# A decoder step on one Trainium2 core: the input projection as one object across five attention stages

## The reference, cut to what matters

```python
u = rms_norm(x, lp['norm_g'][0])
nq, nkv, ngate, sz, sxbc, sdt, dqkv, mg = split_in(u @ lp['w_in'])   # one combined projection
# A: native sparse attention (compressed, selected, window) from nq, nkv, ngate
# B: Mamba-2 SSD mixer from sz, sxbc, sdt;   C: dilated window attention from dqkv
gates = jax.nn.sigmoid(mg.reshape(B, T, 3, D_MODEL))
mix = (gates[:, :, 0] * o_a + gates[:, :, 1] * o_b + gates[:, :, 2] * o_cc) @ lp['w_out']
```

## The kernel before

| stage | dense units before | what runs beside it |
|---|---|---|
| cmp | 36 (NSA columns) | compression of the caches |
| nsas | 72 (dilated columns) | sparse attention of the samples |
| dilp | 36 (SSD columns) and 27 (gates) | dilated attention of the prompt, cache copies |
| ssd | 18 (gates) | SSD mixer in 9 chunks, after a set-up of its own, cache copies |
| nsap | 27 (gates) | sparse attention of the prompt, small copies |

## Time and profile before

### The profile page before, as it was taken

One profiled execution on the slowest core, in us unless ns is written; L12 is line 12 of the kernel. 1 busy time (PEld: TensorE's weight loads), 2 busy tenths in 40 slices (PEclk: granted clock), 3 DMA queues, 4 the chain that ended last, 5 costly groups with the idle time before them and its releaser, 6 DMA issues. The chain is left out here.

```text
span 4517.3 us, 40132 instructions
## 1 busy us (share of the span) xinstructions
PE 3375.6 (75%) x13663; PEld 2097.3 (46%) x13663; DVE 1168.4 (26%) x2988; ACT 698.1 (15%) x1690; POOL 465.5 (10%) x317
## 2 busy tenths in 40 slices
PE   4699568687999545568887013996824999998999
PEld 2577445455555333234554012643412666665443
DVE  2011001012332155334543122412323232232000
ACT  1011000001111123123332001101102111111000
POOL 0000000000000032210000233010031011110000
PEclk7799779898999778679898555997656999999999
DMA  3443232313322258431000533322024111112100
GB/s 105 82 99 69 71 90 75 102 48 118 88 81 68 62 168 278 157 89 32 19 30 25 197 134 110 122 98 69 5 95 143 40 38 38 38 38 93 64 28 12
DMA packets 334815, 374.57 MB, mean 83 GB/s; under 512 B 57633, under 2 KB 297378, under 8 KB 330999
## 3 DMA queue, kind: packets, MB, share of 16 engines
q1 hardware_dynamic: 318162, 308.06, 22.8%
q10 hardware_dynamic: 16478, 64.32, 4.3%
HBM read 313.53 MB, written 115.44 MB: 95 GB/s over the span
## 5 line engine op out<-in xcount | busy, mean ns | idle before, releaser
L225 PE MATMUL d_ps<-d_w,mixer_u_T 128*128 128x288 f32 (+4 forms) x2304 | 675.2, 444 | 90.2 <-ACT d_ob L245 43.3
L2615 PE MATMUL ffn_ps<-up_u_T,ffn_w 128*128 128x352 f32 x2112 | 633.0, 461 | 0.0
L225 PEld LDWEIGHTS d_ps<-d_w,mixer_u_T 128*128 128x128 f32 (+1 forms) x2304 | 423.0, 191 | 276.2 <-issue 50.7
L2615 PEld LDWEIGHTS ffn_ps<-up_u_T,ffn_w 128*128 128x128 f32 x2112 | 400.7, 191 | 220.6 <-issue 2.0
L229 PE MATMUL d_ps<-mixer_u_T,d_w 128*128 128x352 f32 x1152 | 405.8, 499 | 19.0 <-DMA d_w<-w_in 19.0
L2496 PE MATMUL down_ps<-down_w,feed_g_T 128*128 128x512 f32 (+1 forms) x792 | 343.3, 596 | 17.9 <-DMA down_w<-ffn_w_down 17.9
L229 PEld LDWEIGHTS d_ps<-mixer_u_T,d_w 128*128 128x128 f32 x1152 | 225.0, 206 | 145.5 <-issue 44.4
L2496 PEld LDWEIGHTS down_ps<-down_w,feed_g_T 128*128 128x128 f32 (+1 forms) x792 | 144.4, 183 | 216.2 <-issue 198.0
L245 DVE COPY d_ob<-d_ps 128x352 f32<-128x352 f32 (+6 forms) x107 | 52.5, 491 | 444.6 <-PE d_ps L225 185.3
L2675 DVE TENSOR_SCALAR ffn_c<-ffn_h,ffn_now 128x1072 f32<-128x1072 f32 x44 | 36.8, 837 | 449.9 <-ACT ffn_h L2643 449.9
L2412 PE MATMUL mix_B<-gates_o_T,mix_wb 128*128 128x352 f32 x480 | 144.9, 466 | 10.3 <-DMA mix_wb<-w_br_c 10.3
(11 more groups left out here) (423 smaller groups left out, 3639.4 us busy)
## 6 DMA issues: line engine op xcount, KB each, us to landing
out_dil_sample<-cache_dil_w ACTq DMA_DIRECT2D x8, 4088.0 KB
ffn_w<-ffn_w_up SPq DMA_DIRECT2D x44, 512.0 KB, 4.8
cmp_rows<-cache_nsa_kv SPq DMA_DIRECT2D x128, 128.0 KB
dils_kv<-cache_dil_w SPq DMA_DIRECT2D x16, 1024.0 KB, 20.3
graw<-d_ob SPq DMA_DIRECT2D x72, 176.0 KB, 1.8
mix_gate<-graw SPq DMA_DIRECT2D x24, 528.0 KB, 5.6
d_w<-w_in SPq DMA_DIRECT2D x24, 512.0 KB, 6.7
dils_qb<-proj SPq DMA_DIRECT2D x3, 4096.0 KB, 23.2
```

What stands on the lines that cost most here:

```text
L225: mm = pe.matmul(ps[u % 2][0:rows, 0:cols], u_T[:, k, r0:r0 + rows], view(i)[:, k, :], start=(k == 0), stop=(k == DK - 1))
L2615: mm = pe.matmul(ps[u][:, 0:chunk], w[:, slot, k, a, :], u_T[:, k, x * chunk:(x + 1) * chunk], start=(k == 0), stop=(k == DK - 1))
```

## The change

- One object `Dense` holds the weights' slots, the ring, the PSUM tiles, the semaphores and the list of all 216 units; `lane(n)` hands out the next n units to a stage. Its load of the next block goes on over the end of a stage.
- A dense unit is 8 steps (each matmul a step) in place of 2.
- A gate block is 2 blocks of 128 columns (2 DMAs, 6 units), not 3 (3 DMAs, 9 units).
- Units by stage: 36, 72, 36, 36, 36 in place of 36, 72, 63, 18, 27.
- The programs of SP and POOL are run to their first `yield` ahead of all steps, so each attention lane's first loads stand ahead of dense in the queue. One `yield` more in each of these programs keeps the rest in place.
- The attention lane's steps take 0.1 to 0.98 in nsas and 0.08 to 1 in dilp and nsap; cmp and ssd stay at 0 to 1.

```diff
-    def turns(eng, programs):
+    def turns(eng, programs, early=False):
         own = [program(eng) if program else iter(()) for program in programs]
+        if early:
+            for program in own:
+                next(program, None)
...
-            turns(pool, [lane.pool for lane, _, _ in plan])
+            turns(pool, [lane.pool for lane, _, _ in plan], True)
...
-            turns(sp, [lane.sp for lane, _, _ in plan])
+            turns(sp, [lane.sp for lane, _, _ in plan], True)
...
+class Dense:
...
+    RING = 4
...
+        self.units = [(i, j) for i, (kind, _, _) in enumerate(parts) for j in range(9 if kind == "proj" else 6)]
+        self.first = [self.units.index((i, 0)) for i in range(len(parts))]
...
+        else:
+            for x in range(2):
+                m, b = divmod(a + x, 3)
+                sp.dma_start(self.view(i)[:, :, x, :], self.w_gate[:, :, b, m * P:(m + 1) * P]).then_inc(self.w_in[i % 2], 16)
...
+    def lane(self, n_units):
+        lo, hi = self.taken, self.taken + n_units
+        self.taken = hi
...
+                if j == 0:
+                    pe.wait_ge(self.w_in[i % 2], self.landed[i])
+                if u >= 2:
+                    pe.wait_ge(self.copied[u % 2], u // 2)
...
+                    if k < DK - 1:
+                        yield
+                mm.then_inc(self.product, 1)
+                yield
...
+        def sp_program(sp):
+            if lo == 0:
+                self.load(sp, 0)
+            yield
+            for u in range(lo, hi):
+                i, j = self.units[u]
+                if j == 1 and i + 1 < len(parts):
+                    if i >= 1:
+                        sp.wait_ge(self.product, self.first[i])
+                    self.load(sp, i + 1)
+                if u > lo:
+                    self.store(sp, u - 1)
+                for _ in range(DK):
+                    yield
...
-        with Stage(nc, "d0") as st, Stage(nc, "cmp") as own:
-            together(nc, (dense_lane(nc, st, u_T, ins, proj, graw, nsa_cols), 0, 0.8),
...
-        with Stage(nc, "d2") as st, Stage(nc, "dilp") as own:
-            together(nc, (dense_lane(nc, st, u_T, ins, proj, graw, ssd_cols + gates[0:3]), 0, 1),
-                     (dil_prompt_lane(nc, own, ins, proj, o_dil, ident), 0, 1),
...
+        parts += [("gate", q, P) for q in range(0, 3 * DK, 2)]
+        with Stage(nc, "d") as d_st:
+            dense = Dense(nc, d_st, u_T, ins, proj, graw, parts)
+            with Stage(nc, "cmp") as own:
+                together(nc, (dense.lane(36), 0, 0.8), (compress_lane(nc, own, ins, proj, kc_T, vc, ident), 0, 1))
+            with Stage(nc, "nsas") as own:
+                together(nc, (dense.lane(72), 0, 1),
+                         (nsa_sample_lane(nc, own, ins, proj, kc_T, vc, o_cmp, o_sel, o_win, ident), 0.1, 0.88))
+            with Stage(nc, "dilp") as own:
+                together(nc, (dense.lane(36), 0, 1), (dil_prompt_lane(nc, own, ins, proj, o_dil, ident), 0.08, 0.92),
+                         (copies_lane(kept[0:17], moved), 0, 1))
+            ssd(nc, ins, outs, proj, y_b, ident, [(dense.lane(36), 0, 1), (copies_lane(kept[17:], moved), 0, 1)])
+            with Stage(nc, "nsap") as own:
+                together(nc, (dense.lane(36), 0, 1), (nsa_prompt_lane(nc, own, ins, proj, kc_T, vc, oa_T, ident), 0.08, 0.92),
+                         (copies_lane(moves, moved), 0, 1))
```

More of the change, by code:

```diff
@@ L152, in _ @@
         def _(pool):
-            turns(pool, [lane.pool for lane, _, _ in plan])
+            turns(pool, [lane.pool for lane, _, _ in plan], True)
         @block.sync
         def _(sp):
-            turns(sp, [lane.sp for lane, _, _ in plan])
[L160 to L183, removed]
-        if kind == "proj":
[L185 to L193, removed]
@@ L194, in load @@
         if kind == "proj":
-            sp.dma_start(view(i), w_k[:, :, a:a + n]).then_inc(w_in[i % 2], 16)
+            sp.dma_start(self.view(i), self.w_k[:, :, a:a + n]).then_inc(self.w_in[i % 2], 16)
         else:
[L197 to L204, removed]
+            for x in range(2):
+                m, b = divmod(a + x, 3)
+                sp.dma_start(self.view(i)[:, :, x, :], self.w_gate[:, :, b, m * P:(m + 1) * P]).then_inc(self.w_in[i % 2], 16)
@@ L205, in store @@
+    def store(self, sp, u):
+        i, j = self.units[u]
+        kind, a, n = self.parts[i]
+        rows, cols = self.shape(u)
+        sp.wait_ge(self.copied[u % 2], u // 2 + 1)
         if kind == "proj":
             r0 = TILES[j][0]
-            sp.dma_start(proj[r0:r0 + rows, a:a + n], ob[0:rows, u % ring, 0:n]).then_inc(stored[u % ring], 16)
+            sp.dma_start(self.proj[r0:r0 + rows, a:a + n], self.ob[0:rows, u % self.RING, 0:n]).then_inc(self.stored[u % self.RING], 16)
         else:
-            b, c = divmod(j, 3)
@@ L210, in store @@
[L210 to L231, removed]
-                    yield
-            mm.then_inc(product, 1)
-            yield
@@ L236, in copy_out @@
[L236 to L265, removed]
+            x, c = divmod(j, 3)
@@ L1663, in chunks @@
             return program
-        lane = Lane(5 * (CH + 1), chunks(pe_chunk), chunks(act_chunk), chunks(dve_chunk), chunks(pool_chunk), sp_program)
+        lane = Lane(5 * (CH + 1), chunks(pe_chunk), chunks(act_chunk), chunks(dve_chunk), chunks(pool_chunk, True), sp_program)
         together(nc, (lane, 0, 1), *beside)
@@ L2939, in decoder_step @@
-        with Stage(nc, "d3") as st:
-            ssd(nc, ins, outs, proj, y_b, ident,
-                [(dense_lane(nc, st, u_T, ins, proj, graw, gates[3:5]), 0, 1), (copies_lane(kept[17:], moved), 0, 1)])
-        with Stage(nc, "d4") as st, Stage(nc, "nsap") as own:
-            together(nc, (dense_lane(nc, st, u_T, ins, proj, graw, gates[5:]), 0, 1),
-                     (nsa_prompt_lane(nc, own, ins, proj, kc_T, vc, oa_T, ident), 0, 1),
-                     (copies_lane(moves, moved), 0, 1))
+        parts = [("proj", C_Q + i * (C_Z // 4), C_Z // 4) for i in range(4)]
@@ new lines, in decoder_step @@
+        parts += [("proj", C_DIL + i * ((C_MG - C_DIL) // 8), (C_MG - C_DIL) // 8) for i in range(8)]
+        parts += [("proj", C_Z + i * ((C_DIL - C_Z) // 4), (C_DIL - C_Z) // 4) for i in range(4)]
+        parts += [("gate", q, P) for q in range(0, 3 * DK, 2)]
[13 more added lines that the diff above has]
+                         (copies_lane(moves, moved), 0, 1))
```

77 lines of the change are left out of this document (67 added, 10 removed).

## The result

| | before | after |
|---|---|---|
| median (lowest to highest), runs | 4518.12 us (4515.36 to 4524.65), 4 | 4349.49 us (4348.52 to 4352.14), 4 |
| span of the profiled execution | 4517.3 us | 4350.3 us |
| mean granted clock | 0.85 | 0.867 |

The ratio is 0.9626 (95% interval 0.9609 to 0.9642), 169 us faster. The forecast was 4372, with a range of 4290 to 4450.

A forecast was written before the change was run, and what follows sets the result against it. The prediction took PE as the bound in dilp, something else in ssd, and SP's loads in nsas. Stage terms -153 (dilp), +36 (ssd), -27 (nsap) and 0 sum to -144 from 4519.3: 4375, 4372 as median, range 4290 to 4450.

The forecast's parts named there:

- 128 us for the units: In dilp, 27 gate units leave, 54 half units of 2.37 us, all counted as gain because PE is the bound.
- The fine steps, -11 in the sum: In dilp, single dense matmuls between attention steps cover most waits before values, a gain of 11 us.
- The late start, -14: At dilp's start, 23 dense matmuls stand first and hide the attention's loads, a gain of 14 us.
- +5 a chunk: In ssd, dense matmuls in the gaps lengthen each chunk by 3.5 to 7.2 us, taken as 5; eight chunks, +40.
- 3.8 if the clock stays up, since PE's idle time falls to 4 us: In ssd, the gap in front of `ssd_R` takes 3.8 us with its dense matmuls, or 7.6 if the clock drops.
- The late rows: In ssd, slower chunks spread the copies that fill DMA, so rows come less late: -10 us, between 0 and -25.
- the DMA rival: In ssd, three weight loads come 25 us late because copies fill DMA: 75 us more, 4447 us; chance 18%.
- The +43 for the units: In nsap, 9 more gate units, 72 matmuls of 0.59 us, add 43 us.
- +15 - 19 + 9 - 5: In nsas: later SP load +15, dense ahead -19, less dense hidden later +9, tail hiding stores -5; sum 0.
- The clock rival: In dilp, the clock falls to 1.2 GHz with single matmuls: +270 us, 4640 us, slower; chance 4%.
- Dense keeps its price: Fine steps fill nothing: waits of nsap and dilp stay, nsas loses its 20 us; -50, 4466 us; chance 8%.
- More hidden: ssd's chunks grow only 3.5 us, its late rows vanish, nsap gains 65: about -215, 4300 us; chance 15%.

The follow-up runs named there:

- e1: The kernel before with only the units reshared among dilp, ssd and nsap, keeping its two-step lanes and nine-unit gate blocks: 4482.43 us, ratio 0.9942.
- e2: The changed kernel with two steps of four matmuls to a dense unit instead of eight of one: 4438.38 us, ratio 0.9834 to the kernel before.
- e3: The changed kernel with the attention lanes of nsas, dilp and nsap begun at 0 again: 4349.31 us, ratio 0.9642 to the kernel before.
- e10: The changed kernel with two steps to a dense unit in ssd alone, eight elsewhere: 4330.61 us, ratio 0.9592 to the kernel before.
- e7: The changed kernel with the cache copies of ssd moved into nsap: 4391.16 us, ratio 0.9730 to the kernel before.
- e5: The changed kernel with attention lanes from 0 and five slots in the ring: 4334.30 us, ratio 0.9597 to the kernel before.
- e9: The changed kernel with a whole dense unit of eight matmuls as one step: 4591.23 us, ratio 1.0160 to the kernel before.
- e6: The changed kernel with each stage's first weights loaded at that stage's start, not over the border: 4363.91 us, ratio 0.9671 to the kernel before.
- e8: The changed kernel with units 36, 90, 36, 27, 27, more in nsas: 4341.12 us, ratio 0.9624 to the kernel before.
- e12: The changed kernel with five ring slots, nsas attention from 0 and two steps to a unit in ssd: 4307.19 us, ratio 0.9554 to the kernel before.

## Why the prediction was right, and where only its sum was

Each stage's sum has the right sign where one was forecast, but in dilp and ssd it came out close because errors cancelled, which is luck.

**dilp (-153, measured -145).** The sum is right, and its split is not. "Nothing but PE is near its limit, so I count all of it", 128 us for the units, fails alone: e1 gives 89, with more of the tasks' waits uncovered and the clock at 0.91. In the changed kernel PE's busy time falls by 111 (451.0 to 339.7): four gate matmuls cost 2.37 us together, but a single projection matmul between two steps 0.63 to 0.74 each, while four together take 2.18 in e2 (1205.01 to 1207.19, 0.545 each), the price that the forecast used. The fine steps, -11 in the sum, are worth 57 by e2, and 89 and 57 make up the 145 within 1. The late start, -14, got its idle time back and lost it later (e3). A task with three dense matmuls takes 3.36 us (1204.62 to 1207.98), the next, with two, 2.83; the forecast had 3.0 for 2.54. The waits of `dilp_O` are 13.6 us, under the 20 to 30 that were to show it. The stage is 373 us long, not "some 350", because that figure was counted from a window cut at 1528 and not from the 518 us of the whole stage.

**ssd (+36, measured +34).** +5 a chunk was near the warm end of 3.5 to 7.2, and it came near the other: +6.6 (32.2 against a mean of 25.6; the 26.2 of the earlier trace rows is the longer of two kinds of chunk). The step that failed is "3.8 if the clock stays up, since PE's idle time falls to 4 us". PE waits 5.25 us, the clock is at half behind that, and the seven matmuls in front of `ssd_R` take 5.9 to 7.0 us; two steps to a unit, four matmuls behind the wait, take 1.7 us off a chunk (e10). So eight chunks cost 53 us where 40 were counted. The late rows gave 12 us where 10 were counted: before, one chunk took 51.6, 26 over its normal length; now three take 39.3, 36.6 and 34.5, together 14 over 32.2. What brought the sum back is the rest of the stage: set-up and the last chunk, for which +6 was counted, are 6 us shorter (75.2 to 74.2 and 67.2 to 62.1), and no run shows why. That the copies make the rows late is shown by e7. No load of weights came late in ssd (PE never waits for `d_w` there): the DMA rival did not happen.

**nsap (-27, measured -42).** The waits fell by 38 (84 to about 46), less than the 56 counted, and `nsap_S` still waits 39.9 us, where under 25 was to show it. The start gave 22 us of PE's waits (33.0 to 10.6) where 14 were counted. The +43 for the units was mis-sized: PE's busy time rose only by 18 (452.1 over the whole stage before, 470.0), while the clock rose from 0.88 to 0.98. The same matmuls with two steps take 491 us at 0.91 (e2). The three together, -38, -22 and +18, are the 42. The prediction priced waits but not the clock that goes with them.

**nsas (0, measured -6) and cmp (0, measured -9).** PE's stand came, from 504.8 to 549.7 where 530 to 555 was said, so it began earlier (44.9 us). The terms of the forecast, +15 - 19 + 9 - 5, are all effects of the late beginning, and e3 gives +6.7 for them. The fine steps cost another 9 in nsas (e2), and what shortens the stage by 14.6 between e1 and e2 was not separated. That a deeper ring gives only 10 (e5) agrees with SP's loads as the pace. In cmp the finer steps halve the wait for `cmp_rows_T` (14.8 to 7.2 us), which was not looked at; e2 gives 6 of the 9 back.

**The clock rival** had it the wrong way round. It asked whether single matmuls would let the clock fall; e9 shows a clock of 0.74 with whole units, which leave the tasks between them bare. The rule in the Trainium skill, "TensorE: Matmul & The Clock Gate", section "HAM oscillation — how this bites in real kernels", names PE's idle wait for a DMA between tiles as what lets the clock fall, and the trace of ssd agrees for a wait on POOL: behind 5.26 us of it the clock is 0.50. But between the single matmuls of the changed kernel PE does not stand idle, it runs the attention's steps, so that rule does not reach the case to which the prediction applied it. The same page of the Trainium skill, section "A second HAM failure mode: psum-queue depth-cycling", tells of a kernel whose PE "micro-idles between MM groups" often enough for the clock to go up and down; e9's tasks, with waits of 0.5 to 0.9 us each, agree with that. Keeping each run of K whole, as the prediction read the first section, costs 241 us here beside the split (1.0160 against 0.9626). **"Dense keeps its price"** falls with e2: the fine steps bring 94 us. **"More hidden"** was true of nsap alone, and in part (42 of its 65).

What stays open: of the 169 us, 26 are the resharing (e1) and 94 the fine steps (e2). The 49 between e1 and e2 (33 in the stages) are the rest of the change together. The load of weights over the borders has 13 to 20 of them (e6) and the late beginning next to nothing (e3); the first loads of SP and POOL ahead of all steps were never taken out alone. Why nsas is 9 us longer with fine steps is not known. Why the clock falls in e9 with no wait longer than 0.9 us is not settled; the rows show only where.

## What to carry to other kernels

When two lanes share an in-order engine, size the filler's steps so that every gap of the other lane gets one, and count the granted clock as part of the price of a wait. Where a wait of some 5 us cannot be filled, put few matmuls behind it. Measure the price of a unit in each stage by moving some, and stop when a move no longer shows in the time of the whole kernel (e8); and set each stage's step size and beginning by itself (e12).

## What the runs showed of the hardware

The granted clock was low in stretches with short waits only. In e9's dilp PE is busy 436 of 513 us and no wait inside a task is over 0.9 us, and the granted clock is 0.74; cross-attention with 91 of 110 us busy and no wait over 0.6 has 0.50. In the changed kernel's dilp the same tasks, with a dense matmul in most gaps, have 0.98. A dense matmul put between transposes and values, 0.90 us apart without it, made that 0.96. Behind a wait of 5.26 us in ssd seven matmuls took 7.02 us, of which 3 us are seen at a clock of 0.50.
